# A two-layer float32 block on one core: chunked opening, re-interleaved convolutions, and a token-major linear branch

## What is computed

```python
x = x + 0.5 * swiglu_ffn(rmsnorm(x, ffn1_norm), ...)
x = x + hybrid_mixer(rmsnorm(x, mix_norm), ...)   # attention with 3 branches | gated linear attention
x = x + 0.5 * swiglu_ffn(rmsnorm(x, ffn2_norm), ...)
x = rmsnorm(x, final_norm)
```

```python
o = o_intra + o_inter                  # A @ v, and q_in @ S
o_gla = rmsnorm(o_gla, gla_g) * silu(gr)
```

```python
qk = silu(centred_depthwise_conv(concat(q, k), conv_qk_w, conv_qk_b))
merged = sigmoid(g_a + b0) * p_a + sigmoid(g_b + b1) * p_b
out = x + rms_norm(merged @ w_out, norm_post_g)
```

## Time and profile before

| what | us |
|---|---|
| median of 3 runs | 1701.74 (1700.66 to 1703.31) |
| profiled execution, its own time | 1701.64 |
| its span, first to last instruction | 1699.8 |
| PE busy | 1663.9 (98%), weight loads 1346.8 |
| DVE, ACT, POOL busy | 733.6, 645.0, 649.7 |

### The profile page before, as it was taken

One profiled execution on the slowest core, in us unless ns is written; L12 is line 12 of the kernel. 1 busy time (PEld: TensorE's weight loads), 2 busy tenths in 40 slices (PEclk: granted clock), 3 DMA queues, 4 the chain that ended last, 5 costly groups with the idle time before them and its releaser, 6 DMA issues.

```text
span 1699.8 us, 22370 instructions
## 1 busy us (share of the span) xinstructions
PE 1663.9 (98%) x7892; PEld 1346.8 (79%) x7892; DVE 733.6 (43%) x1168; ACT 645.0 (38%) x963; POOL 649.7 (38%) x276
## 2 busy tenths in 40 slices
PE   7999999999999999999999999999999999999997
PEld 6888888888887668888888888878877788887885
DVE  5333330215437755333332033678769631653322
ACT  5233321333335663332232123573544532434432
POOL 3444444443341013444444444443323224444444
PEclk9999999999999999999999999999999999999999
DMA  4222232334221002232223223222111112332232
GB/s 167 101 95 99 99 98 87 99 114 146 83 79 50 2 1 87 87 99 98 90 96 99 97 88 112 87 87 75 62 62 63 64 59 99 112 102 90 92 99 87
DMA packets 41955, 149.26 MB, mean 88 GB/s; under 512 B 4784, under 2 KB 4912, under 8 KB 41648
## 3 DMA queue, kind: packets, MB, share of 16 engines
q1 hardware_dynamic: 40112, 142.36, 25.1%
q10 hardware_dynamic: 1792, 6.19, 1.1%
HBM read 145.39 MB, written 2.10 MB: 87 GB/s over the span
## 4 chain that ended last, share of the span: by engine, by line
PE 62%; issue 24%; POOL 7%; DVE 6%; ACT 1%; DVEq 0%; DMA 0%; POOLq 0%; SPq 0%; ACTq 0%
PE ps L508 14%; PE ps L510 14%; PE ps L509 14%; POOL w_lo L469 6%; PE ps L592 2%; PE ps L591 2%; PE ps L590 2%; PE ps L745 1%; PE ps L759 1%; PE ps L769 1%; DVE scr L2014 1%; PE ps L1008 1%; PE ps L1098 1%; PE ps L1096 1%; PE ps L1097 1%
## 5 line engine op out<-in xcount | busy, mean ns | idle before, releaser
L469 POOL TENSOR_TENSOR w_lo<-w_raw,w_hi 128x1024 fp32r<-128x1024 f32 x262 | 636.6, 2430 | 939.2 <-ACT w_hi L1132 930.9
L1132 ACT ACTIVATE w_hi<-w_raw 128x1024 fp32r<-128x1024 f32 x260 | 275.6, 1060 | 892.7 <-PE ps L510 651.6
L508 PE MATMUL ps<-h_hi,w_hi 128*128 128x512 f32 x1048 | 410.7, 392 | 1.6 <-POOL w_lo L469 0.6
L509 PE MATMUL ps<-h_lo,w_hi 128*128 128x512 f32 x1048 | 408.2, 389 | 0.0
L510 PE MATMUL ps<-h_hi,w_lo 128*128 128x512 f32 x1048 | 407.9, 389 | 0.0
L508 PEld LDWEIGHTS ps<-h_hi,w_hi 128*128 128x128 f32 x1048 | 196.7, 188 | 46.1 <-issue 2.5
L510 PEld LDWEIGHTS ps<-h_hi,w_lo 128*128 128x128 f32 x1048 | 196.7, 188 | 41.5
L509 PEld LDWEIGHTS ps<-h_lo,w_hi 128*128 128x128 f32 x1048 | 196.8, 188 | 40.2
L508 PE MATMUL ps<-n_hi,w_hi 128*128 128x512 f32 x512 | 206.3, 403 | 0.7 <-POOL w_lo L469 0.7
L510 PE MATMUL ps<-n_hi,w_lo 128*128 128x512 f32 x512 | 202.7, 396 | 0.0
L509 PE MATMUL ps<-n_lo,w_hi 128*128 128x512 f32 x512 | 202.2, 395 | 0.0
(11 more groups left out here) (317 smaller groups left out, 1863.0 us busy)
## 6 DMA issues: line engine op xcount, KB each, us to landing
w_raw<-in_units SPq DMA_DIRECT2D x262, 512.0 KB, 3.3
x<-in_x SPq DMA_DIRECT2D x4, 512.0 KB, 6.0
w<-in_w ACTq DMA_DIRECT2D x1, 2048.0 KB, 8.1
out<-scr SPq DMA_DIRECT2D x8, 256.0 KB, 2.0
scr<-proj ACTq DMA_DIRECT2D x8, 128.0 KB, 3.1
inv_count<-in_inv_count ACTq DMA_DIRECT2D x1, 1024.0 KB, 5.0
const<-in_const SPq DMA_DIRECT2D x1, 770.0 KB, 9.7
q_sc<-in_row_const ACTq DMA_DIRECT2D x1, 512.0 KB, 3.5
```

Of the source, the lines that this page charges most:

```text
L469: nc.gpsimd.tensor_tensor(w_lo[:, slot, :], w_raw[:, slot, :], w_hi[:, slot, :].bitcast(F32), ALU.subtract).then_inc(w_lo_done, 1)
L508: nc.tensor.matmul(ps[:, bank, :], whi, hi[:, k, :], start=(n == 0), stop=False)
L509: nc.tensor.matmul(ps[:, bank, :], whi, lo[:, k, :], start=False, stop=False)
L1132: nc.scalar.activation(w_hi[:, slot, :], w_raw[:, slot, :], ACT.Copy).then_inc(w_hi_done, 1)
```

## The change

On each engine the numbers of lines move with the edit; names below are those of the code.

- **Opening.** The second weight unit is loaded right behind the first. ACT rounds both units before chunk 2 of x. PE takes units 0 and 1 together, chunk by chunk (`first_pair`).
- **Compressed heads.** 31 compressed positions become 32, the last one masked. `turn_compressed` transposes four heads of a group at once (128x128), 8 transposes; `pc_t` is written by one copy on DVE and one on ACT, and the value side `vc_tok` is repeated at four partition offsets (two more small copies on ACT).
- **Linear branch.** Intra and inter products swap operands, so that the output has tokens in rows. ACT squares with accumulation, four instructions a tile; `linear_sums` and `linear_spread` go; the root moves from step 26 to step 23 and the inverse from 26 to 24; DVE copies the output out; POOL multiplies it by the inverse root (4 instructions of 128x512, which stand between the projection's last tails and the `h_lo` of the linear heads); PE transposes it at m = 26 to 29 (`linear_turn`, 16 transposes); DVE applies gain and SiLU from `ps`.
- **Convolutions.** ACT makes the centre tap from `ps` (`centre`), DVE the other four; `convolve(2)` stands behind step 3, `convolve(3)` behind step 5; `activate` moves on ACT.
- **Waits at the end.** The first group-product unit no longer waits for SiLU(z); `y_lo` is waited for chunk by chunk there and in `merge_a`. `output` reorders the last two k. POOL adds 4 pieces and DVE 4, its adds between the scalings.

```diff
-            stream(2)
-            stream(4)
             weights(1)
+            stream(2)
+            stream(4)
...
+            pool.wait_ge(grstd_done, 1)
+            for tt in range(TT):
+                own = o_tok[:, tt, :].rearrange("p (h d) -> p h d", h=GH)
+                pool.wait_ge(o_copied, tt + 1)
+                nc.gpsimd.tensor_tensor(own, own, g_col[...].to_broadcast([P, GH, GDV]), ALU.mult).then_inc(go_scaled, 1)
...
+                        four = c_score[:, qt, g * HPG:(g + 1) * HPG, :].rearrange("p h n -> p (h n)")
+                        mm = nc.tensor.transpose(ps[:, 4 + g, qt * P:(qt + 1) * P], four, ident)
...
-                        mm = nc.tensor.matmul(ps[:, HALF_BANK + half, at:at + GC], state[r, m, n % 2, :],
-                                              q_in[r, m, n * GC:(n + 1) * GC], start=False, stop=False,
+                        mm = nc.tensor.matmul(ps[ck, HALF_BANK + half, at:at + P], q_in[r, m, n * GC:(n + 1) * GC],
+                                              state[r, m, n % 2, :], start=False, stop=False,
...
+                    for h, m, half in HEADS_OF:
+                        nc.scalar.activation(square_junk[:, k * P:(k + 1) * P], ps[:, HALF_BANK + half, at:at + P], ACT.Square,
+                                             accum_out=g_col[:, tt * GH + k:tt * GH + k + 1]).then_inc(gsq_done, 1)
...
-                    if m == 26:
+                    if m == 23:
                         linear_root()
...
+                def centre(j):
+                    act.wait_ge(unit_done, U_HEADS + HEAD_UNITS * h + j + 1)
+                    if core or j >= 2:
+                        act.wait_ge(qk_done, 4 * h + j - 1)
+                    nc.scalar.activation(scr[:, 2 + j % 2, :], ps[:, head_bank(j, core), :], ACT.Copy,
+                                         scale=p_("conv_w")[:, bass.ds(at, 1)])
                     if j < 4:
                         if j >= 2:
-                            act.wait_ge(conv_done, 4 * h + j - 1)
+                            activate(j - 2)
+                        centre(j)
...
-                    if 2 <= j < 6:
-                        activate(j - 2)
+                    if 5 <= j < 7:
+                        activate(j - 3)
...
-                run(units, (convolve, 1), (convolve, 2))
+                run(units, (convolve, 1))
                 run(core, (step, 2), (step, 3))
+                run(units, (convolve, 2))
+                run(core, (step, 4), (step, 5))
                 run(units, (convolve, 3))
-                run(core, (step, 4), (step, 5), (step, 6), (step, 7), (roots,))
+                run(core, (step, 6), (step, 7), (roots,))
...
+                    if half == 1 and n >= POOL_ADDS:
+                        for done in (n - 1, n):
```

More of the change, by code:

```diff
@@ L806, in linear_intra @@
                         at = O_AT + m * P
[L807 to L808 removed]
+                        mm = nc.tensor.matmul(ps[:, HALF_BANK + half, at:at + P], intra[:, half, m, :],
+                                              gv_tok[:, tt, h * GDV:(h + 1) * GDV], start=(m == 0), stop=False, skip_group_check=True)
                     mm.then_inc(i_used, 1)
@@ L1039, in merge_a, with two @@
             def merge_a():
-                with pe.Fori(0, DC // 2) as i:
+                def two(i, chunks=None):
                     for j in range(2):
@@ L1044, in merge_a @@
                         tile_unit(unit(U_PA + 2 * j, 4, i), 4 + 2 * j, n_hi, n_lo)
-                        pe.wait_ge(y_lo_done, 3 * DC)
-                        tile_unit(unit(U_PA + 2 * j + 1, 4, i), 5 + 2 * j, y_hi, y_lo)
+                        tile_unit(unit(U_PA + 2 * j + 1, 4, i), 5 + 2 * j, y_hi, y_lo, chunks if j == 0 else None)
+                two(0, lambda k: (y_lo_done, 2 * DC + k + 1))
+                with pe.Fori(1, DC // 2) as i:
+                    two(i)
             def pooled():
@@ new lines, in output @@
+                    if tt == 0:
+                        pe.wait_ge(w_lo_done, u + 1)
+                        pe.wait_ge(m_lo_done, k + 1)
+                    if k == 0 and tt >= 2:
+                        pe.wait_ge(mg_done, 2 * DC + tt - 1)
+                    tok = slice(tt * P, (tt + 1) * P)
+                    for half in range(2):
+                        acc, at = ps[:, 2 * tt + half, :], slice(half * T, (half + 1) * T)
+                        nc.tensor.matmul(acc, m_hi[:, k, tok], w_hi[:, slot, at], start=(k == 0), stop=False)
+                        nc.tensor.matmul(acc, m_lo[:, k, tok], w_hi[:, slot, at], start=False, stop=False)
+                        mm = nc.tensor.matmul(acc, m_hi[:, k, tok], w_lo[:, slot, at], start=False, stop=(k == DC - 1))
```

282 lines of the change are left out of this document (138 added, 144 removed).

## The result

The changed kernel takes 1682.99 us (1681.94 to 1684.86, 4 runs) against 1702.53 of the kernel before (1700.66 to 1704.45, 4 runs): a ratio of 0.988, 95% interval 0.9868 to 0.9892. Forecast were 1686.9 us and a range of 1680.5 to 1692.5. The profiled execution took 1682.85, with a span of 1681.06, 18.71 shorter than the 1699.77 of before.

A forecast was written before the change was run, and what follows sets the result against it. PE was taken to bound the kernel, busy 1663.9 of 1699.8 us. The terms -0.3 - 2.5 - 3.3 - 5.3 - 2.4 - 0.9 = -14.7 took 1701.64 to 1686.9 us, range 1680.5 to 1692.5.

The forecast's parts named there:

- Opening: Start of the kernel: unit 2 starts earlier but DVE's sum leaves little gain; -0.3 us, range -1.0 to +1.4.
- Compressed heads: Transposes between units: eight in about 0.9 us replace 32 in 3.5; -2.5 us, range -2.2 to -2.7.
- Attention: Linear branch in attention: less PE work, partly lost to new waits; -3.3 us, range -8 to +2.
- -5.7 of PE's own work: Attention: sums of squares (3.8) and spreads (4.5) removed, transposes (1.9) and swapped operands (0.7) added.
- +3.2 of waits (5.8 less the old 2.6): Attention: new root wait 3.5, squares 0.3 and 1.0, POOL 1.0, against the old 2.57 us wait for DVE's scaling.
- -0.8 of clock (+1.5 less 2.3): Attention: half-clock loss of 2.3 us behind the old wait goes; a new fall costs 1.5 (0 to 4).
- POOL's 1.0: Attention: POOL's four 128x512 multiplications run while DVE scales, +1.0 us; up to 5.2 by the port rule.
- The squares' 1.3: Attention: ACT's four squaring instructions a tile delay the next exponential, +0.3 for early steps and m = 22, +1.0 at m = 16.
- Rival C: Transposes hold PE's clock at half from the root to the end of attention: 1692.1 us; chance 0.06.
- mLSTM heads: Step 2 ahead of convolution 2 removes PE's wait in heads 2 and 3, 2.7 us each; -5.3 us.
- Group products: Group products and `merge_a`: chunk-wise waits remove PE's waits of 1.84 and 0.53; -2.4 us, range -1.8 to -2.9.
- End: Tail behind PE's last matmul: shorter by one addition's difference, last addition 5.9 instead of 6.8 behind; -0.9 us.

## Why the prediction was right, and where not

**Right in sum.** PE bounds the kernel before and after, and each term of the sum has the right sign. The forecast was 14.7 below the profile of before, it became 18.8. But three terms have their sign by a wrong reading (opening, heads, end), and attention has its size by errors that cancel.

**Opening** (-0.3, measured -1.01 in the profiles). The chain that I worked out to 23.1 was the one that held unit 2 (23.16). The step that failed is the reading that DVE's sum was the later end, with 1.66 us between it and unit 2. Of these, 0.85 were PE's own unit 1 and 0.81 the column sums; nothing waited for DVE. So this chain was no ground for taking only 0.3 of the 1.0. In twelve profiles the new opening reaches unit 4 at 28.8 to 29.3 where the clock stays up behind the column sums, and at 30.5 to 30.9 in the five where it falls there (at 23.1 to 24.5); the old one at 30.00 and 31.20.

**Compressed heads** (-2.5, measured -2.68 in their stage and +0.4 in the one ahead). The mechanism was right: eight transposes take 0.78 us, where 0.9 was forecast. Not foreseen: 2.0 us in untouched products.

**Attention** (-3.3, measured -3.1 at equal clock). The agreement is luck: errors cancel. My -3.3 was -5.7 of PE's own work, +3.2 of waits (5.8 less the old 2.6) and -0.8 of clock (+1.5 less 2.3). Measured are about -4.6, +1.5 and, at equal count of stretches, 0. The new waits are 2.07 at the root, of which 1.84 go when the root goes, and 1.30 at step 29, which neither the root nor POOL makes: PE stands there where before it had a spread of 1.0 us to do, so a part of the spreads' time that I took off in full was cover. POOL's 1.0 is 0.15. The squares' 1.3 wasn't tried by a run; the small waits around m = 16 and 22 are some 0.7 longer than before. Two half-clock stretches, which I reckoned at 2.3, are worth 2.8 there (112.33 less 109.55). The rule of the Trainium skill (page "SBUF — State Buffer", section "Who interferes with whom"), that of DVE and GpSimd the one that issues first keeps the other off the shared ports for its whole instruction, agrees with the trace: the two scalings take 2.25 us beside POOL, 0.74 without, and each ends 0.15 us behind the end of one of POOL's passes (603.64 and 604.69, against 603.49 and 604.54). The time that I worked out by it doesn't follow, since DVE then stands idle for ACT in any case. Rival C didn't come: attention has two half-clock stretches where before had three, and the eight transposes of the compressed heads run at clock 1.00, 0.78 us in all. That the full clock doesn't engage for transposes, as the page "TensorE: Matmul & The Clock Gate" of the Trainium skill has it in "Part 4: PE-mode transpose", these eight don't bear out. Whether transposes by themselves would hold the clock up, no run here shows.

The table load is the price that mattered. It is 1.28 us and the root follows it after 0.01 (600.49, 601.78). The Trainium skill, page "ScalarE: Activation LUTs", section "What ACT_TABLE_LOAD costs", gives 1283 ns for the load, as measured here, and 1380 ns more for a drain, which this trace doesn't show.

**mLSTM heads** (-5.3, measured -5.71 with a half-clock stretch, -6.9 against the kernel with both edits undone and none). The place, the wait and its end were right. The step that failed is the cause of the gain: I gave it to step 2 standing ahead of convolution 2. Either edit alone removes this wait, and the one I counted as an aside, one pass of five less on DVE for each convolution, does all of it. Two convolutions on four passes are 1.7 us shorter (0.86 a pass), and PE waited 1.1. The new order adds nothing that could be measured once the tap is gone.

**Group products** (-2.4, measured -2.94, upper end -2.9): the pick-up after two waits was 0.6, which the range had at its end and the sum not. With the waits put back, the stage is 36.00 again.

**End** (-0.9, measured -2.67). The last addition ends 5.8 behind PE's end, as forecast (5.9), instead of 6.8. But it does so by the new order of k, not by the 4 and 4 additions, which alone let it end later. The step that failed is that the term stopped at the last addition: from there to the end of the span it is 4.1 us before and 2.5 after, and these 1.6 weren't in the sum. They come with both edits. Before, the last three pieces were ready within 2 us of each other; why they then take longer to write, no run tried.

**The clock** was the term that no part of the sum had. It took 1.6 us behind the compressed scores and 1.5 in the first head, and gave 1.3 back in attention.

## What to carry to other kernels

Before crediting a moved instruction with a gain, look at how much shorter the same edit makes the work in front of the waiting engine: here one DVE pass of five less did all that the reordering was made for. A slowed engine costs nothing where it next waits for a third one; follow the wait back to the instruction that has no idle time in front of it (here ACT's table loads) before pricing a contention. Before taking an engine's end for a bound, look whether the engine behind it stood idle: PE had no wait behind DVE's sum. And compare stages at the same number of half-clock stretches, since a median of a few runs moves by several us with them.

## What the runs showed of the hardware

- The places where the clock falls are nearly the same in all these kernels, but in a given run each may or may not be taken. Behind the 64 small score products it fell in 6 of 13 profiles with them in one piece (for 3.41 or 6.83 us; 6 of 11 with 32 columns, 0 of 2 with 31, too few to tell the two apart), behind the 28 small matmuls ahead of the first mLSTM core at 1118 to 1123 in 8 of 14, behind the column sums of the opening in 5 of 12 with the new opening. Ahead of each of these PE did small matmuls (64x32, 64x4 and 128x1; behind the last it also stood 1.2 us). One kernel's five runs lie between 1678.6 and 1686.9 us, with a mean clock of 0.998 at the lower and 0.991 at the upper end; only the first was profiled. What decides it in one run stays open.
- A stretch of 3.41 us at half clock costs 1.5 to 1.7 us under dense products and 1.5 in attention, but next to nothing where it lies on PE's waits: with a third one from 605.1 on (the kernel with the old waits and order of k) attention takes 108.05, with two 107.98.
- The same weight products are spaced differently in kernels that differ in the compressed heads and so in the addresses of later tensors (116.98 against 116.33 us for the last 20 units). The cause wasn't tried.
- An addition of 128x512 on DVE with both inputs in SBUF takes 0.69 us while POOL stands still and 2.77 where a pass of POOL of 2.61 us lies beside it. At the end two of them take 1.70 and 1.75 beside POOL's additions and 0.68 each behind them.
